# A recurrence stage reordered: a small block inverse cut in two around three product steps, GpSimd's gate steps made to wait, a weight block loaded whole and split earlier

## What is computed

```python
def step(state, inp):
    r_t, w_t, k_t, v_t, a_t, b_t = inp
    sa = jnp.einsum('bhvk,bhk->bhv', state, a_t)
    state = (state * w_t[:, :, None, :] + sa[..., None] * b_t[:, :, None, :]
             + v_t[..., None] * k_t[:, :, None, :])
    return state, jnp.einsum('bhvk,bhk->bhv', state, r_t)
```

## Time and profile before

| what | value |
|---|---|
| median of three runs | 1130.73 us (1130.35 to 1132.53) |
| profiled execution, its own time | 1129.51 us |
| span of the profile | 1127.5 us |
| granted TensorE clock, mean | 0.995 of full speed |
| busy share: TensorE, weight loads, VectorE, ScalarE, GpSimd | 97%, 81%, 72%, 49%, 4% |
| chain that ended last, by engine | TensorE 86%, VectorE 8%, ScalarE 2%, DMA 2%, issue 1% |

### The profile page before, as it was taken

One profiled execution on the slowest core, in us unless ns is written; L12 is line 12 of the kernel. 1 busy time (PEld: TensorE's weight loads), 2 busy tenths in 40 slices (PEclk: granted clock), 3 DMA queues, 4 the chain that ended last, 5 costly groups with the idle time before them and its releaser, 6 DMA issues.

```text
span 1127.5 us, 18637 instructions
## 1 busy us (share of the span) xinstructions
PE 1096.3 (97%) x7454; PEld 914.5 (81%) x7454; DVE 816.5 (72%) x1161; ACT 553.5 (49%) x690; POOL 43.3 (4%) x50
## 2 busy tenths in 40 slices
PE   9999999999999887899999999999999999999998
PEld 7887888889778667787888888798977888989896
DVE  4664544538579795979999987999997977555554
ACT  6545633436455425364334356465554756444443
POOL 0000000000000420101111100000000000000000
PEclk9999999999999989999999999999999999999999
DMA  9585456453344221649989963374540654564633
GB/s 337 192 267 187 152 183 223 157 179 112 113 149 136 74 42 41 260 153 374 341 321 343 347 212 115 111 226 149 167 149 2 202 161 133 177 207 166 208 127 112
DMA packets 138141, 205.86 MB, mean 183 GB/s; under 512 B 19592, under 2 KB 95645, under 8 KB 138078
## 3 DMA queue, kind: packets, MB, share of 16 engines
q1 hardware_dynamic: 130644, 177.63, 47.9%
q0 software_dynamic: 6560, 25.19, 5.9%
q10 hardware_dynamic: 874, 2.15, 0.5%
HBM read 202.33 MB, written 1.57 MB: 181 GB/s over the span
## 4 chain that ended last, share of the span: by engine, by line
PE 86%; DVE 8%; ACT 2%; DMA 2%; issue 1%; ACTq 0%; DVEq 0%
PE ps L749 24%; PE ps L751 24%; PE ps L750 24%; PE ps L975 2%; DVE wl L2532 1%; PE ps L1193 1%; PE ps L1632 1%; DMA raw<-in_ab_w_in 1%; PE ps L826 1%; PE ps L1108 1%; PE ps L1460 1%; PE ps L1107 1%; PE ps L1132 1%; PE ps L1614 1%; DVE wide L2646 1%
## 5 line engine op out<-in xcount | busy, mean ns | idle before, releaser
L2532 DVE TENSOR_TENSOR wl<-raw,wh 128x2048 fp32r<-128x2048 f32 (+2 forms) x154 | 345.4, 2248 | 98.5 <-ACT wh L1755 98.1
L749 PE MATMUL ps<-wh,xh 128*128 128x512 f32 (+3 forms) x856 | 339.0, 396 | 2.7 <-DVE wl L2532 1.4
L751 PE MATMUL ps<-wl,xh 128*128 128x512 f32 (+3 forms) x856 | 332.2, 388 | 0.0
L750 PE MATMUL ps<-wh,xl 128*128 128x512 f32 (+3 forms) x856 | 332.0, 388 | 0.0
L1755 ACT ACTIVATE wh<-raw 128x2048 fp32r<-128x2048 f32 (+2 forms) x154 | 286.7, 1878 | 41.0 <-PE ps L751 31.0
L749 PEld LDWEIGHTS ps<-wh,xh 128*128 128x128 f32 x856 | 161.4, 189 | 39.3 <-issue 2.4
L751 PEld LDWEIGHTS ps<-wl,xh 128*128 128x128 f32 x856 | 161.3, 188 | 34.8
L750 PEld LDWEIGHTS ps<-wh,xl 128*128 128x128 f32 x856 | 161.5, 189 | 33.3 <-issue 1.0
L749 PE MATMUL ps<-wh,gh 128*128 128x512 f32 x288 | 114.1, 396 | 0.8 <-DVE wl L2532 0.8
L751 PE MATMUL ps<-wl,gh 128*128 128x512 f32 x288 | 113.8, 395 | 0.0
L750 PE MATMUL ps<-wh,gl 128*128 128x512 f32 x288 | 113.6, 395 | 0.0
(11 more groups left out here) (448 smaller groups left out, 1307.1 us busy)
## 6 DMA issues: line engine op xcount, KB each, us to landing
wide<-in_w_ada POOLq DMA_DIRECT2D x24, 1024.0 KB, 9.2
raw<-in_ffn_w_gate SPq DMA_DIRECT2D x44, 512.0 KB, 4.4
raw<-in_ffn_w_up SPq DMA_DIRECT2D x44, 512.0 KB, 5.5
raw<-in_ffn_w_down SPq DMA_DIRECT2D x22, 1024.0 KB, 5.0
raw<-in_w_mlp_in SPq DMA_DIRECT2D x16, 1024.0 KB, 7.3
raw<-in_w_mlp_out SPq DMA_DIRECT2D x16, 1024.0 KB, 5.1
raw<-in_w_in SPq DMA_DIRECT2D x16, 512.0 KB, 4.8
raw<-in_w_in SPq DMA_DIRECT2D x8, 1024.0 KB, 5.0
```

The lines of the kernel that those rows point to most:

```text
L749: pe.matmul(o, lh, rh, start=start, stop=False)
L750: pe.matmul(o, ll, rh, start=False, stop=False)
L751: return pe.matmul(o, lh, rl, start=False, stop=stop)
L2532: v.tensor_tensor(wl[:, s, 0:width], raw[:, s, 0:width], f32(wh[:, s, 0:width]), ALU.subtract).then_inc(lo_ready[s], 1)
```

## The change

VectorE's `near` ends with the left product of size 8. The last right product becomes `near_last()`. For head half 0 it follows at once. For head half 1 it comes behind `r4_out(1)`. The four half splits of the first two blocks move: two around `q_out(0)`, two behind `state_out(1)`. GpSimd's second gate steps also wait for `wkv.y1` of group 1. On SyncE `a_columns((2, 3))` goes ahead of `near_out(1)`, and the third block comes whole, in one DMA, without waits on group 2's steps. ScalarE's split of it moves between `gkv_out(2)` and `gkv_out(3)`. The four `near` buffers (3456 bytes per partition) are allocated last, so the buffers that stood behind them start 3456 bytes lower. The arithmetic is the same.

```diff
@@ make_plan
-    for (n, k), s, dmas in zip(O_ORDER, (2, 0, 1, 2), (1, 1, 4, 1)):
+    for (n, k), s, dmas in zip(O_ORDER, (2, 0, 1, 2), (1, 1, 1, 1)):
@@ buffers: near_m, near_u, near_c, near_p
-        (behind h)
+        (behind posi, the last ones)
@@ SyncE, recurrence_loads
                 a_columns((1,))
                 near_out(0)
                 near_in(1)
+                a_columns((2, 3))
                 near_out(1)
-                a_columns((2, 3))
                 sp.wait_ge(S("gate_T"), B("gate_T") + 4)
-                in_pieces(("o",) + O_ORDER[2], 2)
+                in_place(("o",) + O_ORDER[2])
@@ GpSimd
             for hh in range(2):
                 ...
                 pool.wait_ge(S("gate_out"), B("gate_out") + 2 * (hh + 1))
+                if hh:
+                    pool.wait_ge(S("wkv.y1"), B("wkv.y1") + 2)
@@ ScalarE
                 if g == 2:
                     gkv_out(2)
+                    act.wait_ge(S("fold"), B("fold") + 16)
+                    split_in_place(("o",) + O_ORDER[2])
                     gkv_out(3)
                 ...
                 r1_out(g + 1)
-                if g == 2:
-                    act.wait_ge(S("fold"), B("fold") + 16)
-                    split_in_place(("o",) + O_ORDER[2])
                 r2_out(g)
@@ VectorE, end of near(hh)
+                left_product(4)
+                right_product(4)
+                left_product(8)
+
+            def near_last():
+                right_product(8, last=True)
@@ VectorE, order
                 if g == 0:
                     near(0)
+                    near_last()
 ...
                 y1_out(g)
-                if g == 0:
-                    split_in_place(first, 0)
-                else:
+                if g == 2:
                     centre(0, 0)
                 y1_out(g + 1)
                 ...
                 r4_out(g)
-                if g == 0:
-                    split_in_place(first, 1)
-                    split_in_place(second, 0)
-                else:
+                if g == 2:
                     centre(0, 1)
                     variance(0, 0)
                     variance(0, 1)
                 r4_out(g + 1)
                 if g == 0:
-                    split_in_place(second, 1)
+                    near_last()
+                    split_in_place(first, 0)
                 else:
                     gated(0, 0)
                 q_out(g)
-                if g == 2:
+                if g == 0:
+                    split_in_place(first, 1)
+                else:
                     gated(0, 1)
                 q_out(g + 1)
                 if g == 0:
                     inverse_out(2)
                     inverse_out(3)
                 state_out(g)
                 state_out(g + 1)
+                if g == 0:
+                    split_in_place(second, 0)
+                    split_in_place(second, 1)
```

More of the change, by code:

```diff
@@ L333, in build @@
         h = sb("h", [P, NT, D])
[L334 to L337, removed]
         xh, xh_plain = rounded("xh", [P, KT, SEQ])
@@ L359, in build @@
         posi = sb("posi", [P, NT], I32)
+        near_m = sb("near_m", [P, NEAR])
+        near_u = sb("near_u", [P, NEAR])
+        near_c = sb("near_c", [P, 2 * P])
+        near_p = sb("near_p", [P, 64])
         ps = ctx.enter_context(nc.psum_tensor("ps", [P, 8, 512], F32))
@@ L504, in in_place @@
                   .then_inc(raw_loaded[s], 16)
[L506 to L515, removed]
             def recurrence_loads():
@@ L2990, in mask_k, with corners, near_part, small_products @@
                                 mask_two("strict_st", "upto_st"), ALU.mult).then_inc(S("wkv.gk"), 1)
+            def corners(s):
+                k = 8 // s
+                u, m = [t[:, :].rearrange("p (k z) -> p k z", k=k)[:, :, 0:32 * s].rearrange("p k (i c) -> p k i c", c=16) for t in (near_u, near_m)]
+                return u[:, :, 0:s, 0:s], u[:, :, 0:s, s:2 * s], u[:, :, s:2 * s, s:2 * s], m[:, :, 0:s, s:2 * s]
+            def near_part(s):
+                return near_p[:, 0:8 * s].rearrange("p (k i c) -> p k i c", i=s, c=s)
+            def small_products(s, a, b, o):
+                k = 8 // s
+                products = W(8, 0, k * s ** 3).rearrange("p (k i c j) -> p k i c j", k=k, i=s, c=s)
+                for n in range(k):
+                    m = v.tensor_tensor(products[:, n], a[:, n].unsqueeze(2).to_broadcast([P, s, s, s]),
+                                        b[:, n].rearrange("p j c -> p c j").unsqueeze(1).to_broadcast([P, s, s, s]), ALU.mult)
+                link(m)
+                for n in range(k):
+                    m = v.tensor_reduce(o[:, n], products[:, n], AX_X, ALU.add)
+                return m
+            def left_product(s):
+                _, _, u22, m12 = corners(s)
+                link(small_products(s, m12, u22, near_part(s)))
+            def right_product(s, last=False):
+                u11, u12, _, _ = corners(s)
+                m = small_products(s, u11, near_part(s), u12)
+                if last:
+                    m.then_inc(S("wkv.near"), 1)
+                else:
+                    link(m)
             def near(hh):
@@ L2998, in near @@
                     v.wait_ge(S("near_unit"), B("near_unit") + 1)
[L2999 to L3003, removed]
                 _, u12, _, m12 = corners(1)
@@ L3013, in near @@
                 link(v.tensor_tensor(u12[:, :, 0, :], u12[:, :, 0, :], part, ALU.add))
[L3014 to L3024, removed]
-                            m_ = v.tensor_reduce(o[:, n], products[:, n], AX_X, ALU.add)
-                        if s < 8 or o is part:
-                            link(m_)
-                m_.then_inc(S("wkv.near"), 1)
+                left_product(4)
[3 more added lines that the diff above has]
+                right_product(8, last=True)
             def inverse_out(g):
```

## The result

The changed kernel takes **1113.32 us** (median of four runs, 1112.80 to 1115.20), against 1130.54 for the kernel before in the same set: ratio **0.9847** (95% interval 0.983 to 0.9864). That is 17.2 us less. The forecast was 9.3 less, with a range that began at 1119.4: the direction was right, the size and the range were wrong. The profiled run took 1112.97 us, with a span of 1110.9.

A forecast was written before the change was run, and what follows sets the result against it. TensorE, busy 97% of the span, bounds the kernel, so time could come from two holes in the recurrence and the low clock behind them. 4.4 + 4.85 = 9.3 us off the 1130.73 median gave 1121.4 us, range 1119.4 to 1126.

The forecast's parts named there:

- Edits at nothing: Gate steps' hold, moved splits' remainders and new buffer addresses: no effect, with bounds of 0.5 us either way for addresses.
- Part 1: First hole: shorter near(1) lets off_1(0) start at 408.5, 3.75 us earlier, and out_parts(0) 6.2 us earlier, at full clock.
- part 2: Inverse's DRAM passage after the moved right product: 5.1 us; VectorE stands 1.5 us, TensorE 1.2, no fall of the clock.
- rival C: Inverse later, or TensorE's new standing lowers the clock: costs 1.3 to 3 us, time 1122.7 to 1124.4; chance 0.14.
- Part 3: Third block loaded whole lands in 5.1 us; next_state(0, 2) starts 4.4 us earlier, at 426.85.
- rival A: Third block lands late, 8.2 us after its issue, leaving 1.8 of the 4.4 us; time 1124.0; chance 0.2.
- Part 4: Second hole: off_2(2) starts 3.9 us earlier and its result comes 0.95 sooner at full clock, together 4.85 us.
- B: GpSimd is not what slows near(1); off_1(0) 1.8 us later, time 1123.2, or 1125.5 if the clock falls; chance 0.08.
- D: Slower: ScalarE's wait on the third block ahead of gkv_out(3) takes the whole gain; 1132 at 16 us landing; chance 0.03.
- E: Holes move but the stage's end stays, VectorE's work behind 446 us hanging on something unmoved; 1130.7; chance 0.03.

The follow-up runs named there:

- move_only: The kernel before with the four near buffers allocated last and nothing else changed; 1120.64 us, ratio 0.991.
- no_hold: The changed kernel without GpSimd's wait for y1 ahead of its second gate steps; 1115.89 us (one run).
- near_whole: The changed kernel with the last right product back ahead of y1_out(0), GpSimd still held; 1112.17 us (one run).
- block_between: further, but with the third block's load issued behind a_columns((2, 3)) and ahead of near_out(1); 1111.75 us, ratio 0.9837.
- order_only: The changed kernel with the near buffers back in their old place, between h and xh; 1123.76 us, ratio 0.9938.
- pad64: The changed kernel with 64 unused bytes per partition ahead of xh; 1126.31 us (one run).
- pad_all128: The changed kernel with 128 unused bytes ahead of the first tile, so all tiles move together; 1111.20 us (one run).
- early_block: The changed kernel with only the third block's 1 MB load issued ahead of a_columns((2, 3)) and near_out(1); 1116.55 us, ratio 0.988.
- further: The changed kernel with right product between r4_outs, states before inverse spreading, second block's splits around carry, third block issued first, split ahead of h_out(0); 1111.78 us.
- states_first: further without its early block: third block issued last and split between the two gkv_out as in the changed kernel; 1112.77 us, ratio 0.9845.

## Why the prediction was right or wrong

**The failed step is the one under "Edits at nothing":** "The buffers' new addresses change no count, and no row shows a cost of an address: I take zero, bounds 0.5 either way." It is worth 9.7 us alone (move_only), more than the whole forecast. "No row shows a cost of an address" was not true either: the products with `spare` took 390 ns before the change, beside 395 for the same product with `wl`. I had not looked for two paces among products of one shape, and took the absence of a row for a bound. The edit changes an operand's address in 3,240 instructions of 232 ns, two thirds of TensorE's time, and one per cent of that is 7.5 us. Half a microsecond was no bound but a belief.

**Part 1, right.** Near(1) ran at near(0)'s pace (3.53 us against 3.51). Off_1(0) starts at 403.71, which is 408.4 in before's time (4.70 us added; forecast 408.5), and out_parts(0) at 407.79, or 412.5 (forecast 412.3), with a full clock to 418. GpSimd was the cause (no_hold). But these 6 us did not reach the end, and what the cut of near(1) adds to them is taken back in part 2 (near_whole).

**Part 2, right mechanism, one term too small.** wkv.near came at 410.70, in before's time 415.40, the forecast to the digit, by luck: the multiply started 0.2 us later than forecast and ran 0.2 us shorter (1.47 us, not 1.7). The passage through DRAM took 6.0 us instead of 5.1: the two last loads took 2.07 us to issue (block_between 1.28) and landed at 416.69. VectorE stood 2.58 us, not 1.5, TensorE 2.24, not 1.2, and in that stand the clock fell: "so I take no fall of the clock" failed. It was 0.85 in the microsecond from 418 and 0.50 over the next three, and gram_v's 32 products took 1.13 us instead of 0.69. That was rival C's case, priced at 1.3 to 3 us.

**Part 3, 4.4 forecast, 2.9 measured.** The block landed 5.5 us after its issue (forecast 5.1) and ScalarE did not wait for it, so rival A fell. next_state(0, 2) starts at 423.73, 428.4 in before's time, 2.9 us earlier instead of 4.4. The 1.5 us between are part 2's: the inverse was 0.9 us late, and the products behind it ran at the lower clock, so that gkv_out(2), at 420.48, was 1.5 us late in before's time.

**Part 4, 4.85 forecast, 4.0 measured.** off_2(2) follows off_1(2) by 1.93 us, as forecast, at full clock; but its products stand 0.38 us at 433.91 with the mark "issue", and r4_out(2) comes 1.93 us behind its start, not 1.08. In the rows of before, this step had no such stand. The end moves with it, as said: 2.86 + 3.97 = 6.8 us.

**Rivals.** A, B, D and E did not come about. C did, and took 1.5 of the 2.4 us by which the stage missed its sum; the broken off_2(2) took the other 0.9. Without the buffers the result would have been order_only's 1123.8, inside the range: for the order of work the range held; for the edit at nothing it did not.

## What to carry to other kernels

Price an edit that moves buffers by what its operands are used in, and try it alone: put a pad of 64 or 128 bytes ahead of the tile that a large product reads and look at the mean duration in the groups by line. Look there first for products of one shape that run at two paces. A step cut out of a chain saves nothing if its result's own journey becomes the wait; ask when it must leave, not only what stands behind it. Place a 1 MB load behind the moment at which an engine on the path is due new code, and look for the instruction queue in the DMA view where an idle time is marked "issue".

## What the runs showed of the hardware that I had not expected

- **The relative place of two SBUF operands sets the pace of a product.** Products of 128x512 with the weight tile stationary: 232.3 ns from start to start when the moving tile starts 128 bytes off the weights' place modulo 256 (before; 64 bytes off, pad64, has the same durations), 226.7 when it starts at the same (2.4%). Moving both by 128 bytes together changed nothing (pad_all128). The Trainium skill has a page on operands' starts (SBUF — State Buffer, section "Operand start alignment"), but it is about which starts are allowed and says itself that it is not about speed, so the measurement stands alone here.
- **TensorE's code comes over the same DMA engines as the weights,** and TensorE stood 2.3 and 2.6 us for it when 1 MB was issued 2 to 3 us before the code's usual moment (early_block, further; 0.37 to 0.91 in the changed kernel, block_between and states_first). It went on 1.2 to 1.5 us after the packet had ended.
- **A stand of TensorE need not lower its clock.** It fell during the stand from 417.05 to 419.29 in the changed kernel (1.00 up to 418, then 0.85, then 0.50), and behind the 2.57 us stand in further (0.78, then 0.50 over 409 to 412). It stayed at 1.00 behind the 2.32 us stand in early_block, whose products before it were the same. What told these apart no run here shows.
